# Attention B in steps of four units instead of two: values of four units in one row, four slots of turned probabilities, two units to an output bank

## The reference, cut to what matters

```python
r0 = jnp.clip(r - kh // 2, 0, rows - kh)
k_rows = lax.dynamic_slice_in_dim(kg, r0, kh, axis=1)      # kh = 8 rows of 64 columns
sc = einsum(q_row, k_band) * scale
sc = jnp.where(mask, sc + bias, -jnp.inf)
p = jax.nn.softmax(sc, axis=(-2, -1))
o = einsum(p, v_band)                                      # then o * silu(gate), then @ w_out
```

## Time and profile before

| what | value |
|---|---|
| median of 3 timed runs | 1482.88 us (1482.83 to 1483.05) |
| span of the profiled execution | 1480.8 us |
| PE busy in the span | 1438.2 us, 97% |
| PEld busy | 1268.2 us, 86% |
| DVE busy | 801.8 us, 54% |
| ACT busy | 622.0 us, 42% |
| POOL busy | 427.0 us, 29% |
| attention B on PE, first `scores` to first matmul of the output projection | 519.45 to 635.29 us |

### The profile page before, as it was taken

How to read it: one execution, slowest core, us unless ns; L and a number is a source line. 1 busy time by engine, 2 the same in 40 slices (tenths; PEclk the granted TensorE clock), 3 DMA queues, 4 the chain that set the end, 5 groups by cost and what they waited for, 6 DMA issues and landing times.

```text
span 1480.8 us, 30804 instructions
## 1 busy us (share of the span) xinstructions
PE 1438.2 (97%) x12682; PEld 1268.2 (86%) x12682; DVE 801.8 (54%) x1475; ACT 622.0 (42%) x1250; POOL 427.0 (29%) x527
## 2 busy tenths in 40 slices
PE   7999999989999999999999999999998998999998
PEld 7999998867777788888899999888897887888887
DVE  6238310149999878745420723452424776888431
ACT  6323121027777677632432112332335554777210
POOL 0212132110000277622202212221205874434320
PEclk9999999999999999999999999999999999999999
DMA  7313222000000033356325244433121021222342
GB/s 252 65 54 104 97 79 81 16 1 0 1 1 1 19 122 98 80 178 171 93 43 59 50 95 84 61 58 57 29 66 43 27 91 40 67 78 68 100 134 80
DMA packets 88017, 105.32 MB, mean 71 GB/s; under 512 B 25343, under 2 KB 72095, under 8 KB 87880
## 3 DMA queue, kind: packets, MB, share of 16 engines
q1 hardware_dynamic: 87880, 103.36, 26.7%
HBM read 80.20 MB, written 23.12 MB: 70 GB/s over the span
## 4 chain that ended last, share of the span: by engine, by line
PE 57%; DVE 4%; ACT 2%; issue 1%; DMA 1%; POOL 0%; DVEq 0%; SPq 0%; ACTq 0%
PE ps L378 22%; PE ps L1346 12%; PE ps L2851 2%; PE ps L1154 2%; PE ps L1138 2%; PE ps L2837 2%; PE ps L2826 1%; PE ps L2227 1%; PE ps L2170 1%; PE ps L2185 1%; DMA p_w_raw<-w_in 1%; PE ps L1131 1%; PE ps L1133 1%; PE ps L1132 1%; PE ps L2814 1%
## 5 line engine op out<-in xcount | busy, mean ns | idle before, releaser
L344 POOL TENSOR_TENSOR p_w_lo<-p_w_raw,p_w_hi 128x2048 fp32r<-128x2048 f32 (+1 forms) x27 | 127.7, 4728 | 505.7 <-ACT p_w_hi L318 505.7
L378 PE MATMUL ps<-p_w_hi,w_out_hi 128*128 128x256 f32 (+1 forms) x640 | 181.9, 284 | 1.2 <-ACT p_spill L403 1.1
L378 PE MATMUL ps<-p_w_hi,w_out_lo 128*128 128x256 f32 (+1 forms) x640 | 179.7, 281 | 0.0
L378 PE MATMUL ps<-p_w_lo,w_out_hi 128*128 128x256 f32 (+1 forms) x640 | 179.6, 281 | 0.0
L378 PE MATMUL ps<-p_w_hi,hT_hi 128*128 128x256 f32 x576 | 163.7, 284 | 1.5 <-DVE hT_lo L140 1.5
L378 PE MATMUL ps<-p_w_hi,hT_lo 128*128 128x256 f32 x576 | 162.6, 282 | 0.0
L378 PE MATMUL ps<-p_w_lo,hT_hi 128*128 128x256 f32 x576 | 162.6, 282 | 0.0
L378 PEld LDWEIGHTS ps<-p_w_hi,w_out_hi 128*128 128x128 f32 x640 | 120.6, 188 | 2.3 <-ACT p_spill L403 1.6
L378 PEld LDWEIGHTS ps<-p_w_lo,w_out_hi 128*128 128x128 f32 x640 | 120.8, 189 | 0.0
L378 PEld LDWEIGHTS ps<-p_w_hi,w_out_lo 128*128 128x128 f32 x640 | 120.6, 188 | 0.0
L378 PEld LDWEIGHTS ps<-p_w_hi,hT_hi 128*128 128x128 f32 x576 | 109.0, 189 | 1.9 <-DVE hT_lo L140 1.9
(11 more groups left out here) (306 smaller groups left out, 3590.2 us busy)
## 6 DMA issues: line engine op xcount, KB each, us to landing
p_w_raw<-w_in SPq DMA_DIRECT2D x26, 1024.0 KB, 8.0
s_gate<-p_spill SPq DMA_DIRECT2D x48, 128.0 KB, 1.8
kbT<-x SPq DMA_DIRECT2D x8, 512.0 KB, 6.5
b_w_raw<-w_out SPq DMA_DIRECT2D x8, 512.0 KB, 3.4
qT<-s_gate SPq DMA_DIRECT2D x8, 512.0 KB, 6.9
qT<-x SPq DMA_DIRECT2D x8, 512.0 KB, 3.3
s_x<-qT SPq DMA_DIRECT2D x8, 512.0 KB, 3.0
c_table<-s_line SPq DMA_DIRECT2D x8, 512.0 KB, 3.6
```

The source lines that it names most:

```text
L344: ops.tensor_tensor(self.w_lo[:, c % 2, :, 0:w], self.raw[:, :, 0:w], self.w_hi[:, c % 2, :, 0:w].bitcast(F32), ALU.subtract).then_inc(sel ...
L378: last = self.nc.tensor.matmul(out, lhs, rhs, start=(kt == 0 and i == 0), stop=(kt == KT - 1 and i == 2))
```

## The change

- **Steps of four units** (`STEP = 4`). On PE a step is now four `values` in a row, then `turn_probs` of two units, `scores` of two, `turn_probs` of two, `scores` of two.
- **Four slots of turned probabilities.** Slots 2 and 3 lie in columns 768 to 1023 of `g.tok`, which are free in this stage. The two banks of `turn_probs` stay two; so `turn_probs` of the third and fourth unit of a step now waits until the copy of the first and second is done (`wait_emptied(pe, u - 2)`).
- **Two units to an output bank.** The values of units `u` and `u + 2` of a step share bank `6 + u % 2`, in columns 0 to 63 and 64 to 127. `store` waits for all four `values` of its step, and `values` waits for all stores of the step before.
- **The order on DVE**: four stores, `keys_low` if there is one, two bias operations, the copy of the fourth unit, two bias operations, and then `split_lo`, if there is one.
- **The order on ACT**: two copies, `keys_high` if there is one, one exponential, the copy of the third unit, three exponentials, and then `split_hi`, if there is one. All four first exponentials stand ahead of the first copy.
- **The splits of `w_out`** stand in steps 8, 12, 20, 24, 32, 36, 44 and 48 (named by their first unit), both halves of a tile in the same step. `keys_low` stands in steps 4, 20 and 36.

```diff
     n_units = len(units)
     W = NA_KH * GRID_W
     v, v_loaded = front.v, front.v_loaded
-    q_diag, k_hi, k_lo, prob, prob_t = front.q_diag, front.k_hi, front.k_lo, front.prob, front.prob_t
+    q_diag, k_hi, k_lo, prob = front.q_diag, front.k_hi, front.k_lo, front.prob
+    STEP = 4
+    SPLITS = {8: 0, 12: 1, 20: 2, 24: 3, 32: 4, 36: 5, 44: 6, 48: 7}
     k_hi_ready = k.sem("b_k_hi_ready")
     k_lo_ready = k.sem("b_k_lo_ready")
     out = k.sb("b_out", [P, 2, ROWS, HD])
...
         return min(max(r - NA_KH // 2, 0), ROWS - NA_KH)
+    def prob_t(u):
+
+        if u % STEP < 2:
+            return front.prob_t[:, u % STEP, :].rearrange("p (a c) -> p a c", a=2)
+        s = u % STEP - 2
+        return g.tok[:, 2 * s:2 * s + 2, 768:D]
+
+    def sums(u, half):
+
+        return ps[half, 6 + u % 2, u % STEP // 2 * HD:u % STEP // 2 * HD + HD]
+
+    def steps_before(u):
+        return u // STEP * STEP
+
     def value_tile(p, i, r0, j):
         if r0 % 2:
...
         def turn_probs(u):
             pe.wait_ge(prob_ready, u + 1)
+            if u % STEP >= 2:
+                wait_emptied(pe, u - 2)
             for j in range(4):
                 last = nc.tensor.transpose(ps[:, 4 + u % 2, j * P:(j + 1) * P], prob[:, u % 4, j * P:(j + 1) * P], g.ident[:, :])
             last.then_inc(turned, 1)
...
                 pe.wait_ge(last_group, 4)
             if r0 % 2:
                 pe.wait_ge(v_odd_loaded[p % 2], 16 * (p // 2 + 1))
-            if u >= 2:
-                pe.wait_ge(out_stored, 2 * (u - 1))
+            if u >= STEP:
+                pe.wait_ge(out_stored, 2 * steps_before(u))
             for j in range(4):
                 for i in range(2):
-                    last = nc.tensor.matmul(ps[i * HD:(i + 1) * HD, 6 + u % 2, 0:HD],
-                                            prob_t[:, u % 2, j * P + i * HD:j * P + (i + 1) * HD],
+                    at = j % 2 * P + i * HD
+                    last = nc.tensor.matmul(sums(u, slice(i * HD, (i + 1) * HD)), prob_t(u)[:, j // 2, at:at + HD],
                                             value_tile(p, i, r0, j), start=(j == 0), stop=(j == 3))
             last.then_inc(out_ready, 1)
...
         for i in range(4):
             last = nc.tensor.transpose(ps[:, LAST_BANK, i * P:(i + 1) * P], front.last_out[:, i, :], g.ident[:, :])
         last.then_inc(last_group, 1)
-        for u in range(0, n_units, 2):
-            if u >= 2:
-                values(u - 2)
-                values(u - 1)
-            turn_probs(u)
-            turn_probs(u + 1)
-            if u + 4 < n_units:
-                scores(u + 4)
-                scores(u + 5)
+        for u in range(0, n_units, STEP):
+            if u:
+                for n in range(u - STEP, u):
+                    values(n)
+            for n in (u, u + 2):
+                turn_probs(n)
+                turn_probs(n + 1)
+                if n + 4 < n_units:
+                    scores(n + 4)
+                    scores(n + 5)
         pe.wait_ge(max_ready, n_units)
         op.turn(pe, 0)
-        values(n_units - 2)
-        values(n_units - 1)
+        for n in range(n_units - STEP, n_units):
+            values(n)
     def vector(dve):
         def bias_and_max(u):
...
         def empty(u):
             dve.wait_ge(turned, u + 1)
-            if u >= 2:
-                dve.wait_ge(out_ready, u - 1)
-            nc.vector.tensor_copy(prob_t[:, u % 2, :], ps[:, 4 + u % 2, :]).then_inc(pt_by["dve"], 1)
+            if u >= STEP:
+                dve.wait_ge(out_ready, u - STEP + 1)
+            nc.vector.tensor_copy(prob_t(u), ps[:, 4 + u % 2, :].rearrange("p (a c) -> p a c", a=2)).then_inc(pt_by["dve"], 1)
         def store(u):
             p, r = units[u]
             dve.wait_ge(prob_ready, u + 1)
             nc.vector.reciprocal(stat[:, 2, u:u + 1], stat[:, 1, u:u + 1]).then_inc(recip_ready, 1)
             dve.wait_ge(recip_ready, u + 1)
-            dve.wait_ge(out_ready, u + 1)
+            dve.wait_ge(out_ready, steps_before(u) + STEP)
             if r == 0 and p >= 2:
                 dve.wait_ge(pair_sent[p % 2], 32)
-            nc.vector.tensor_scalar(out[:, p % 2, r, :], ps[:, 6 + u % 2, 0:HD], stat[:, 2, u:u + 1],
+            nc.vector.tensor_scalar(out[:, p % 2, r, :], sums(u, slice(0, P)), stat[:, 2, u:u + 1],
                                     None, ALU.mult).then_inc(out_stored, 2)
         def keys_low(p):
...
         bias_and_max(3)
         dve.wait_ge(last_group, 4)
         scaled_heads(nc.vector, g, LAST, front.last_sum[:, :, :]).then_inc(last_group, 1)
-        for u in range(0, n_units, 2):
-            if u >= 2:
-                store(u - 2)
-                store(u - 1)
+        for u in range(0, n_units, STEP):
+            if u:
+                for n in range(u - STEP, u):
+                    store(n)
             if u % ROWS == 4 and u // ROWS + 1 < PAIRS:
                 keys_low(u // ROWS + 1)
-            if u % 6 == 4 and 0 < u // 6 <= KT:
-                ws.split_lo(dve, nc.vector, u // 6 - 1)
-            if emptier(u + 1) == "dve":
-                empty(u + 1)
             if u + 4 < n_units:
                 bias_and_max(u + 4)
                 bias_and_max(u + 5)
-        store(n_units - 2)
-        store(n_units - 1)
+            empty(u + 3)
+            if u + 4 < n_units:
+                bias_and_max(u + 6)
+                bias_and_max(u + 7)
+            if u in SPLITS:
+                ws.split_lo(dve, nc.vector, SPLITS[u])
+        for n in range(n_units - STEP, n_units):
+            store(n)
     def scalar(act):
         def exponentials(u):
...
         def empty(u):
             act.wait_ge(turned, u + 1)
-            if u >= 2:
-                act.wait_ge(out_ready, u - 1)
-            nc.scalar.copy(prob_t[:, u % 2, :], ps[:, 4 + u % 2, :]).then_inc(pt_by["act"], 1)
+            if u >= STEP:
+                act.wait_ge(out_ready, u - STEP + 1)
+            nc.scalar.copy(prob_t(u), ps[:, 4 + u % 2, :].rearrange("p (a c) -> p a c", a=2)).then_inc(pt_by["act"], 1)
         def keys_high(p):
             if p >= 2:
                 act.wait_ge(scores_ready, ROWS * (p - 1))
             front.keys_high(p).then_inc(k_hi_ready, 1)
-        exponentials(0)
-        exponentials(1)
-        for u in range(0, n_units, 2):
-            if u % ROWS == 2 and u // ROWS + 1 < PAIRS:
+        for u in range(STEP):
+            exponentials(u)
+        for u in range(0, n_units, STEP):
+            empty(u)
+            empty(u + 1)
+            if u % ROWS == 0 and u // ROWS + 1 < PAIRS:
                 keys_high(u // ROWS + 1)
-            if u % 6 == 2 and 0 < u // 6 <= KT:
-                ws.split_hi(act, nc.scalar.copy, u // 6 - 1)
-            empty(u)
-            if emptier(u + 1) == "act":
-                empty(u + 1)
-            if u + 2 < n_units:
-                exponentials(u + 2)
-                exponentials(u + 3)
+            if u + 4 < n_units:
+                exponentials(u + 4)
+            empty(u + 2)
+            if u + 4 < n_units:
+                for n in range(u + 5, u + 8):
+                    exponentials(n)
+            if u in SPLITS:
+                ws.split_hi(act, nc.scalar.copy, SPLITS[u])
     return Part(sync, gpsimd, tensor, scalar, vector, {"max_ready": max_ready, "k_lo_ready": k_lo_ready,
                                                        "out_stored": out_stored, "sent": pair_sent, "last_group": last_group}, ws), send
```

## The result

The changed kernel takes 1490.84 us (median of 5, 1488.89 to 1491.25), the one before 1482.95 beside it (5 runs); the ratio is 1.0049, with a 95% interval of 1.0038 to 1.0059. It is slower, by 0.5%, where 1487.7 was forecast: 7.9 us more than before by the medians where 4.8 were expected, and 0.16 us inside the upper end of the stated range. The profiled span is 1488.8 us against 1480.8.

A forecast was written before the change was run, and what follows sets the result against it. PE was taken to bound attention B, busy all 90 us. A gain of 4.7 us less 2.1 at head and tail gives −2.6; stalls add 7.4, so +4.8 on 1482.88: 1487.7 us, own range 1486 to 1490, outer 1480.0 to 1491.0.

The forecast's parts named there:

- leaving scores for transposes costs like leaving values: Rival on PE's new transition in attention B: 3.0 us on top, 1490.7 us; chance 0.08.
- PE's row: PE in attention B: a step of four takes 6.69 against 7.00 us, saving 4.7 us in 15 steps.
- The head: Start of attention B: ACT's first copies come after four exponentials, so PE stands still for 1.3 us.
- The splits: Steps with a split of w_out in attention B: PE is put back by 7.4 us in sum.
- the four pairs: Neighbouring split steps 8 and 12, 20 and 24, 32 and 36, 44 and 48: 1.39, 2.09, 2.52 and 1.39 us lost.
- The loop: ACT and DVE after a split: last exponential to last exponential takes 8.08 us against PE's 6.69.
- waits on the stores: Sign in the changed profile that would show the forecast wrong; no size given.
- The tail: End of attention B: three more stores, 0.45 each, precede the projection; head and tail together eat 2.1 of 4.7 us.
- hidden: Rival on the w_out splits: the loop is below 6.69 us, PE never waits, 1480.3 us; chance 0.13.
- half hidden: Rival on the w_out splits: links overlap by some 0.4 a split, some 4 us are left, 1484; chance 0.17.
- The one without a price at the ends: Rival on attention B: no stalls and no price at head and tail, 4.7 us gained, 1478.2 us; chance 0.07.
- The sum: Whole kernel: −2.6 + 7.4 = +4.8 us, so 1487.7 us; own range 1486 to 1490, chance 0.55.

The follow-up runs named there:

- e3: Changed kernel with ACT's cast of w_out at the head of its step and ACT's first two copies ahead of exponentials 2 and 3; 1480.44 us, ratio 0.9985.
- e1: Changed kernel with ACT's cast of a w_out tile at the head of its step instead of after the last exponential; 1481.89 us, ratio 0.9993.
- e2: Changed kernel with the eight splits in steps 0, 8, 16 to 56, never in neighbouring steps; 1486.15 us, ratio 1.0022.
- e8: Kernel before, steps of two, with cast and subtraction of the splits at the ends of the same step; 1483.18 us, ratio 1.0000.
- e7: As e4, with the first four rows of the last pair of heads sent by themselves a step earlier; 1477.36 us, ratio 0.9961.
- e4: As e3, with DVE's split of the output projection's first tile ahead of its last four stores; 1478.60 us, ratio 0.9968.
- e9: Changed kernel with ACT copying the third unit before the step's first exponential instead of after it; 1488.71 us, ratio 1.0038.
- e6: Kernel before with values on weights of 128 columns instead of 64, the second head's output left wrong; measured once, 1556.8 us.

## Why the prediction was right, point by point

Two things first about the number. Its mechanism held, but 1490.84 lies above the 1486 to 1490 that the forecast gave itself, and the outer range, up to 1491.0, held by 0.16 us: two of the five runs, 1491.02 and 1491.25, lie beyond it, so that much is luck. And the number alone would have pointed to the wrong rival: *leaving scores for transposes costs like leaving values* said 1490.7. The trace refutes it, with 0.23 at that place and plain steps of 6.69 on average.

**PE's row.** Right: 6.69 forecast for a plain step, 6.68 and 6.70 measured, with 0.23 from scores to transposes. In fourteen steps that is 14 × 6.70 = 93.8 us of 101.4; the rest is stalls.

**The head.** Right: 1.3 us of waiting forecast, 1.24 measured; the first values came 9.39 us after the first scores for 9.29. e3 shows the order of the four exponentials to be its cause.

**The splits.** Right in mechanism and in size. Forecast for the four pairs were 1.39, 2.09, 2.52 and 1.39; the steps' excess over 6.70 gives 0.52 + 0.91 = 1.43, 1.22 + 0.88 = 2.10, 1.65 + 0.88 = 2.53 and 0.71 + 0.90 = 1.61, in sum 7.67 for 7.4. The loop was put at 8.08 and measured 8.04. That it was the cause is shown by e1, which takes the cast out of the loop and gets all of it back; that it takes two in a row, or one and a `keys_low`, by e2; that it takes the long step, by e8. Two details differ. The forecast named waits on the stores as a sign of being wrong. They came, 1.0 us in all, but as a part of this loop, since the stores stand behind the late subtraction and e1 removes these waits with the rest. And the last pair cost 0.22 more than forecast: DVE stands still for 0.19 us between its second and third store there, for which the profile names no releaser, so this stays open.

**The tail.** Here the term was too small. I had the projection 10.3 us after `values(56)`; it came after 11.9 (643.02 − 631.12). I had costed DVE's three stores, and they are there as forecast (2.88 from the first store to the projection for 2.90), but I left out that `op.turn(0)` needs the mixed tile, and with it the chain of last stores, send, load and POOL's multiplication. In steps of four those stores run late, and PE waits 1.22 us. e7 sends the first rows a step sooner, which removes this wait, and the stage shrinks by 1.5 us.

**The rivals.** The splits were not hidden, nor half hidden, and the new transition had no price. The first two would have shown as absent or halved waits, the third as longer plain steps. The one without a price at the ends falls by e3 and e4.

**The sum.** −2.6 + 7.4 became −2.6 + 0.1 + 0.1 + 1.6 + 7.7 = +6.9 in the stage; the ratio says +7.3 (5.6 to 8.7). The direction and the range held; the miss is the tail, the term that was sized too small by 1.6 us.

## What to carry to other kernels

When work is regrouped into longer steps, follow each filler (a cast, a subtraction) around the loop that it closes between two engines, by every path (e9 took one out and the other was as long), and compare the loop with the bound engine's step, not the engines' busy shares: here DVE at 0.83 of PE's time and ACT at 0.75, read before the change, still made a loop of 8.04 us against 6.70. Put the producer of a filler at the head of its engine's step and the consumer at the end of the other's; that one move was worth 8 us of stage. The grouping itself was good for some 4.7 us (15 steps at 0.31) and gave some of it back at the two ends, where what follows must be rearranged with it.

## What the runs showed of the hardware

The gaps around `values` belong to the shape of its matmuls: with weights of 128 x 64 in halves of the array, `values` pays about 0.3 us a visit, and with weights of 128 x 128 nothing (e6). The Trainium skill, "TensorEngine Tiling (Array Packing)", section "Key Properties", says that changing the tiling mode drains the engine, and the trace agrees for this place; in attention A the trace has the same two weight shapes by turns without a gap, so it is not every change of shape that costs, and which do was not tried.

The halves were worth far more than the gaps: 32 records took 1.15 us in halves and 3.68 with wide weights, a pace of 0.028 against 0.110 us, almost a factor of four. The single records of the traces split it: the narrow ones start in pairs, 0.006 us apart, a pair every 0.058 us, and the wide ones singly, one every 0.11 us. So a factor of two lies in the pairs and 1.9 in the time of one; what sets that time was not tried.
